# The residual addition on TensorE: an ordinary f32 matmul with a scaled diagonal in place of a transpose, and 1/ALPHA taken out of the branches

## The reference

```python
x = layer_norm(ALPHA * x + y, ln_mix_g[l], ln_mix_b[l])   # y: HGRN2 + convolution, or pooling
x = layer_norm(ALPHA * x + y, ln_xa_g[l], ln_xa_b[l])     # y: attention to a memory
x = layer_norm(ALPHA * x + y, ln_ffn_g[l], ln_ffn_b[l])   # y: swiglu
# ALPHA = 4 ** 0.25, layer_norm with an epsilon of 1e-5
```

## Time and profile before

| | |
|---|---|
| three runs | 1280.35, 1280.9, 1282.54 us, median 1280.9 |
| profiled execution | 1280.35 us, its span 1278.4 us |
| mean granted clock of PE | 0.996 |
| busy | PE 1258.9, DVE 829.3, ACT 661.1, POOL 27.6 us |
| instructions | 17136, of which 6788 matmul records of PE |
| read from HBM | 215.71 MB, 170 GB/s over the span |

### The profile page before, as it was taken

One profiled execution on the slowest core, in us unless ns is written; L12 is line 12 of the kernel. 1 busy time (PEld: TensorE's weight loads), 2 busy tenths in 40 slices (PEclk: granted clock), 3 DMA queues, 4 the chain that ended last, 5 costly groups with the idle time before them and its releaser, 6 DMA issues.

```text
span 1278.4 us, 17136 instructions
## 1 busy us (share of the span) xinstructions
PE 1258.9 (98%) x6788; PEld 1084.9 (85%) x6788; DVE 829.3 (65%) x1270; ACT 661.1 (52%) x999; POOL 27.6 (2%) x32
## 2 busy tenths in 40 slices
PE   9999999999999999999999999999999999999997
PEld 7888888898788888899989897888888997888886
DVE  5655666868667565667998665755557564755554
ACT  6454546657474444454525654644444654644443
POOL 0000000010000000000000000000001000000000
PEclk9999999999999999999998999999999999999999
DMA  8655555552355555554424542755555442655551
GB/s 288 216 184 182 182 189 189 166 181 83 104 181 186 183 192 185 185 173 151 152 83 149 193 137 88 260 189 190 192 186 165 165 149 83 217 195 189 189 185 62
DMA packets 61854, 217.87 MB, mean 170 GB/s; under 512 B 6608, under 2 KB 9936, under 8 KB 61264
## 3 DMA queue, kind: packets, MB, share of 16 engines
q1 hardware_dynamic: 61488, 216.29, 50.2%
q10 hardware_dynamic: 288, 0.49, 0.1%
HBM read 215.71 MB, written 1.05 MB: 170 GB/s over the span
## 4 chain that ended last, share of the span: by engine, by line
PE 90%; DVE 7%; ACT 1%; DMA 1%; issue 0%; SPq 0%; POOL 0%; DVEq 0%; ACTq 0%
PE bank L1920 27%; PE bank L1922 26%; PE bank L1921 26%; DVE arena L1740 3%; DVE w_lo L1117 2%; PE bank L2122 2%; PE bank L2259 1%; PE bank L2219 1%; PE bank L1942 1%; DMA w_raw<-weights_d 1%; PE bank L2230 1%; PE bank L2008 0%; PE bank L2042 0%; PE bank L2251 0%; PE bank L2213 0%
## 5 line engine op out<-in xcount | busy, mean ns | idle before, releaser
L1117 DVE TENSOR_TENSOR w_lo<-w_raw,w_hi 128x1024 fp32r<-128x1024 f32 x383 | 467.2, 1225 | 340.7 <-ACT w_hi L584 339.4
L584 ACT ACTIVATE w_hi<-w_raw 128x1024 fp32r<-128x1024 f32 x383 | 403.8, 1058 | 473.4 <-PE bank L1922 453.3
L1920 PE MATMUL bank<-w_hi,x_hi 128*128 128x512 f32 (+2 forms) x928 | 360.3, 388 | 2.9 <-DVE w_lo L1117 2.4
L1922 PE MATMUL bank<-w_hi,x_lo 128*128 128x512 f32 (+2 forms) x928 | 355.8, 383 | 0.0
L1921 PE MATMUL bank<-w_lo,x_hi 128*128 128x512 f32 (+2 forms) x928 | 355.6, 383 | 0.0
L1920 PEld LDWEIGHTS bank<-w_hi,x_hi 128*128 128x128 f32 x928 | 174.5, 188 | 37.4 <-DVE w_lo L1117 3.5
L1922 PEld LDWEIGHTS bank<-w_hi,x_lo 128*128 128x128 f32 x928 | 174.4, 188 | 34.0
L1921 PEld LDWEIGHTS bank<-w_lo,x_hi 128*128 128x128 f32 x928 | 174.6, 188 | 32.6
L1920 PE MATMUL bank<-w_hi,h_hi 128*128 128x512 f32 (+1 forms) x364 | 142.4, 391 | 0.0
L1922 PE MATMUL bank<-w_hi,h_lo 128*128 128x512 f32 (+1 forms) x364 | 141.3, 388 | 0.0
L1921 PE MATMUL bank<-w_lo,h_hi 128*128 128x512 f32 (+1 forms) x364 | 141.2, 388 | 0.0
(11 more groups left out here) (314 smaller groups left out, 1425.7 us busy)
## 6 DMA issues: line engine op xcount, KB each, us to landing
w_raw<-weights_d SPq DMA_DIRECT2D x395, 512.0 KB, 3.3
arena<-weights_d SPq DMA_DIRECT2D x4, 512.0 KB, 6.1
arena<-ln_rows_d SPq DMA_DIRECT2D x2, 1024.0 KB, 5.6
arena<-late_d SPq DMA_DIRECT2D x1, 1056.0 KB, 5.7
xs<-x_d SPq DMA_DIRECT2D x2, 512.0 KB, 6.1
kv_mem<-mem_d SPq DMA_DIRECT2D x1, 1024.0 KB, 8.7
out_d<-xs SPq DMA_DIRECT2D x4, 256.0 KB, 2.4
cst<-cst_d SPq DMA_DIRECT2D x1, 671.0 KB, 6.9
```

Source lines behind the costliest of these rows:

```text
L584: nc.scalar.activation(w_hi[:, slot(b), :], w_raw[:, b % RAW, :], ACT.Copy).then_inc(hi_ready, 1)
L1117: nc.vector.tensor_tensor(w_lo[:, slot(b), :], w_raw[:, b % RAW, :], w_hi[:, slot(b), :].bitcast(F32), ALU.subtract).then_inc(lo_ready, 1)
L1920: nc.tensor.matmul(out, wh, xh, start=start, stop=False, skip_group_check=True)
L1922: return nc.tensor.matmul(out, wl, xh, start=False, stop=stop, skip_group_check=True)
```

## The change

`residual` and the pooling branch use an ordinary f32 matmul with `res_i`, the identity times ALPHA, as moving operand. DVE makes `res_i` once at the start, and PE waits for it once, ahead of branch 5. All divisions by ALPHA go, with the two columns and their semaphore, and the epsilon is the plain one everywhere. The tensor `scaled` (16 columns) goes and `res_i` (128 columns) comes in its place in SBUF.

```diff
--- before.py
+++ after.py
@@ -188,7 +188,7 @@
         h_lo = sb("h_lo", [P, 8, S], F32R)
 
         tokst = sb("tokst", [P, 76])
-        scaled = sb("scaled", [P, 16])
+        res_i = sb("res_i", [P, P])[:]
         ident = sb("ident", [P, P])[:]
 
         kv_mem = sb("kv_mem", [P, 4, DC * S])
@@ -224,7 +224,6 @@
         row_sum = [small[:, 8 + 4 * k:12 + 4 * k] for k in range(2)]
         lam_e, lam_p, neg_lam = small[:, 16:18], small[:, 18:20], small[:, 20:21]
         g_q_scaled, g_sub_scaled = small[:, 21:22], small[:, 22:23]
-        hg_over, pool_over = scaled[:, 0:4], scaled[:, 4:12]
         lb_e, lb_t, lower, upper = small[:, 28:40], small[:, 40:44], small[:, 44:48], small[:, 48:52]
         decay = small[:, 56:88]
 
@@ -354,8 +353,8 @@
             "xt_ready xt_ps ss_ready rs_ready dg_ready rb_ps rb_ready")
         raw_in = [sem(f"raw_in{k}") for k in range(RAW)]
         hi_ready, lo_ready, block_done, vec_chain = sems("hi_ready lo_ready block_done vec_chain")
-        res_ready, xh_ready, xl_ready, y_ready, na_ready, nd_ready, xn_ready, xd_ready, over_alpha = sems(
-            "res_ready xh_ready xl_ready y_ready na_ready nd_ready xn_ready xd_ready over_alpha")
+        res_ready, xh_ready, xl_ready, y_ready, na_ready, nd_ready, xn_ready, xd_ready, id_scaled = sems(
+            "res_ready xh_ready xl_ready y_ready na_ready nd_ready xn_ready xd_ready id_scaled")
         lat_sq, var_ready, lat_norm, lat_t, lat_hi, lat_lo, v_up, vup_evac, dv_evac = sems(
             "lat_sq var_ready lat_norm lat_t lat_hi lat_lo v_up vup_evac dv_evac")
         dq_sq, dq_sum, dq_n, dq_t, dq_evac, dk_sq, dk_n, dk_t, dk_evac = sems(
@@ -768,7 +767,7 @@
                         done(b)
                         nc.scalar.activation(v_mem[l][:, :, c * S:(c + 1) * S],
                                              fill_bank(l, m, c)[:, :].rearrange("p (t n) -> p t n", n=S),
-                                             ACT.Copy, scale=1.0 / ALPHA).then_inc(mem_evac, 1)
+                                             ACT.Copy).then_inc(mem_evac, 1)
 
             def exponentials(n, head):
 
@@ -1068,12 +1067,11 @@
             blk()
             ln_norm(7, 1)
             mem_blocks(1, 8, 9)
-            act.wait_ge(over_alpha, 1)
             for c in range(DC):
                 act.wait_ge(pool_ps, 2 * (c // 4) + c % 2 + 1)
                 if c % 4 >= 2:
                     act.wait_ge(pool_lo, c - 1)
-                nc.scalar.activation(x_hi[:, c, :], pooled(c), ACT.Copy, scale=pool_over[:, c:c + 1]).then_inc(pool_hi, 1)
+                nc.scalar.activation(x_hi[:, c, :], pooled(c), ACT.Copy, scale=col("ln_g", LN_COL[7] + c)).then_inc(pool_hi, 1)
             for k in range(4):
                 act.wait_ge(xt_ps, 16 + 4 * LN[7] + k + 1)
                 x_pair(7, k)
@@ -1408,8 +1406,7 @@
             def ln_stats(v, t):
                 link(ln_part(v, 1, t))
                 link(nc.vector.bn_aggr(ln_mv[t], ln_bn[t]))
-                eps = LN_EPS if v in (7, 10) else LN_EPS / ALPHA ** 2
-                nc.vector.tensor_scalar(ln_var[:, t:t + 1], ln_mv[t][:, 1:2], eps, None, ALU.add).then_inc(var_ready, 1)
+                nc.vector.tensor_scalar(ln_var[:, t:t + 1], ln_mv[t][:, 1:2], LN_EPS, None, ALU.add).then_inc(var_ready, 1)
 
             def ln_norm(v, t):
 
@@ -1545,8 +1542,8 @@
             mark(nc.vector.tensor_scalar(g_q_scaled, col("g_diff_q"), SCALE_DIFF, None, ALU.mult))
             mark(nc.vector.tensor_scalar(g_sub_scaled, col("g_diff_sub"), 1.0 - LAMBDA_INIT, None, ALU.mult))
 
-            mark(nc.vector.tensor_scalar(hg_over, col("hg_g", 0, 4), 1.0 / ALPHA, None, ALU.mult))
-            nc.vector.tensor_scalar(pool_over, col("ln_g", LN_COL[7], DC), 1.0 / ALPHA, None, ALU.mult).then_inc(over_alpha, 1)
+            dve.wait_ge(x_in[0], 32)
+            nc.vector.tensor_scalar(res_i, ident, ALPHA, None, ALU.mult).then_inc(id_scaled, 1)
             token_ffn(0, FIRST["ffn1"])
             blk()
             token_rstd(1)
@@ -1848,7 +1845,7 @@
 
             for h in range(HG_HEADS):
                 dve.wait_ge(ho_bc, h // 2 + 1)
-                nc.vector.scalar_tensor_tensor(ho[:, h, :], ho[:, h, :], hg_over[:, h:h + 1], half(1 - h // 2, h),
+                nc.vector.scalar_tensor_tensor(ho[:, h, :], ho[:, h, :], col("hg_g", h), half(1 - h // 2, h),
                                                ALU.mult, ALU.mult).then_inc(hy_f, 1)
 
             for h in range(HG_HEADS):
@@ -1858,8 +1855,7 @@
             for k in range(CC + 1):
                 if k < CC:
                     dve.wait_ge(conv_ln, k + 1)
-                    nc.vector.scalar_tensor_tensor(conv[:, k, :], conv[:, k, :], 1.0 / ALPHA, conv_sig_buf[:, k, :],
-                                                   ALU.mult, ALU.mult).then_inc(cy_f, 1)
+                    nc.vector.tensor_tensor(conv[:, k, :], conv[:, k, :], conv_sig_buf[:, k, :], ALU.mult).then_inc(cy_f, 1)
                 if k:
                     c = k - 1
                     dve.wait_ge(cy_hi, c + 1)
@@ -1881,10 +1877,9 @@
             token_ffn(2, FFN3)
             blk()
             mem_blocks(8, 9)
-            dve.wait_ge(over_alpha, 1)
             for c in range(DC):
                 dve.wait_ge(pool_hi, c + 1)
-                low_gain(x_lo[:, c, :], pooled(c), pool_over[:, c:c + 1], x_hi[:, c, :], pool_lo)
+                low_gain(x_lo[:, c, :], pooled(c), col("ln_g", LN_COL[7] + c), x_hi[:, c, :], pool_lo)
             mem_blocks(9, 10)
             mark(ln_part(8, 0, 0))
             ln_stats(8, 0)
@@ -2005,8 +2000,8 @@
 
                 for t in range(2):
                     for c in range(4 * h, 4 * h + 4):
-                        nc.tensor.matmul(PB[banks[t]][:, c % 4 * P:c % 4 * P + P], xs[:, c, 0, t * P:(t + 1) * P], ident,
-                                         start=False, stop=False, is_transpose=True, skip_group_check=True)
+                        nc.tensor.matmul(PB[banks[t]][:, c % 4 * P:c % 4 * P + P], xs[:, c, 0, t * P:(t + 1) * P], res_i,
+                                         start=False, stop=False, skip_group_check=True)
 
             def token_turns(blocks, outs, chunks, hi, lo, start, stop, first=None, ready=None, between=None, ahead=0):
 
@@ -2573,6 +2568,7 @@
                     ins = nc.tensor.transpose(half(4 + c // 2, c)[:, t * P:(t + 1) * P], xs[:, c, 1, t * P:(t + 1) * P], ident)
                 if c % 2:
                     ins.then_inc(conv_t, 1)
+            pe.wait_ge(id_scaled, 1)
             token_out(5, AB_OUT, "ab_out", lambda c: pe.wait_ge(hy_lo, c + 1) if c < 4 else pe.wait_ge(cy_lo, c - 3), lambda i: None)
             mem_blocks(1, 6, 7)
             ln_turn_halves(5)
@@ -2614,8 +2610,8 @@
                         ins.then_inc(block_done, 1)
                 pe.wait_ge(xn_ready, XN[7] + DC)
                 for c in range(DC):
-                    ins = nc.tensor.matmul(PB[Z_BANK[8][c // 4][t]][:, c % 4 * P:c % 4 * P + P], xs[:, c, 0, s], ident,
-                                           start=False, stop=c % 4 == 3, is_transpose=True, skip_group_check=True)
+                    ins = nc.tensor.matmul(PB[Z_BANK[8][c // 4][t]][:, c % 4 * P:c % 4 * P + P], xs[:, c, 0, s], res_i,
+                                           start=False, stop=c % 4 == 3, skip_group_check=True)
                 ins.then_inc(zt_ps, 1)
             nb[0] += 2
             mem_blocks(1, 10, 14)
```

## The result

The changed kernel takes 1287.16 us in the median (1286.42 to 1287.82, 5 runs) against 1280.35 us for the kernel before in the same set of runs (1278.85 to 1282.54, 5 runs). The ratio is 1.0055, with a 95% interval of 1.0042 to 1.0069: slower, by 6.8 us in the medians. The forecast was 1288.2 us, range 1285.5 to 1290.5. The profiled execution of the changed kernel took 1286.86 us; its span is 1284.8 us. Ten further executions of the changed kernel are on record and in none of these figures: nine lie between 1285.22 and 1290.64 us, and one took 5632.21 us, for which I have no cause.

A forecast was written before the change was run, and what follows sets the result against it. The prediction took PE, busy 98% of the span, as the bound. Eight residual groups add 7.3 us, all other terms nothing: 1280.35 + 7.3 = 1287.65, plus 0.55 to the runs' median, 1288.2 us, range 1285.5 to 1290.5.

The forecast's parts named there:

- The unit: PE's residual additions: 8 ordinary matmuls take 1.78 us against 0.87 for 8 transposes, 0.91 extra a group, 7.3 for eight.
- The prediction's lower bound: PE's residual matmuls: a record can hardly be cheaper than 0.106 us, so 64 more cost at least 6.8 us.
- All on the path: All eight residual groups lie on PE's part of the chain, from 699.29 to 1063.71 us, so 7.3 us counts in full.
- Nothing back: PE's longer waits after 699 us, 3.5 us for x_lo and 3.2 for ACT, shift without shrinking; nothing is regained.
- Rival A: PE waits less for x_lo after the first group and regains up to 3.5 us, giving 1284.7 us; chance 0.06.
- The rule: Skill pages: FP32 transpose mode four times as fast, true FP32 matmul four passes; the prediction set a trace factor of two against it.
- Rival B: Residual matmuls on PE cost four transposes each, 20.9 us more, giving 1301.8 us; chance 0.03.
- DVE and ACT: Making the diagonal, dropped small operations and constants, convolution products and gains change the time by nothing, 0.12 us if cover is gone.
- rival D: The arena's move makes the convolution's taps on DVE cheaper, so the kernel is faster, for example 1277.2 us; chance 0.03.
- the sum: Whole kernel: 1280.35 + 7.3 = 1287.65 us for the profiled execution, 1288.2 for the median.
- a sign against it: The prediction is wrong if the span before 699 us, ahead of the first residual group, moves.

The follow-up runs named there:

- Experiment 1: Kernel before with only the 64 residual transposes made ordinary f32 matmuls with the plain identity; 1286.45 us, ratio 1.0048.
- experiment 3: Changed kernel with each of the 64 ordinary residual matmuls issued twice; 1300.6 us, ratio 1.0161 to the kernel before.
- experiment 4: Changed kernel with the residual matmuls in f32r, 128 wide, on a tile of the memory's high part (wrong tensor added); 1279.52 us, ratio 0.9998 to the kernel before.
- experiment 2: Changed kernel with the 64 residuals put back to transposes with the identity, the rest of the change kept; 1279.64 us, ratio 1.0002 to the kernel before.
- Experiment 5: Kernel before, no edit, run again for a second profile; 1278.32 us, one run.
- experiment 7: Changed kernel with 12 spare matmuls at the end and 8 and 5 in two waits for w_lo in the convolution's stretch; 1286.42 us, ratio 1.0059 to the kernel before.
- experiment 8: Kernel before, with its transposes, plus spare matmuls at the end and in two convolution waits; 1277.69 us, ratio 0.9995.
- experiment 6: Changed kernel with 12 spare 128x128 f32 matmuls in PE's wait at the end; 1286.31 us, ratio 1.0061 to the kernel before.

## Why the prediction was right

**The unit.** 8 ordinary matmuls at 1.78 us against 8 transposes at 0.87 was read from one stretch of another line and holds to the hundredth on the residual lines. Experiment 1 shows that this edit makes the cost, experiment 3 that it adds up (0.223 for a further one), and experiment 4 that one record of 128 columns in f32r costs no less than a transpose. The prediction's lower bound, that a record can hardly be cheaper than 0.106 us, is too general: in the same trace the 14 records of L2527, on 32 partitions, take from 654.18 to 654.83 us, 0.046 each. For the residuals, which fill 128 partitions, it holds.

**All on the path.** The eight groups lie on the chain at 1.78 us each, but for the first of the pool branch (2.05 for 1.08 before), the statistics of branch 5 stand 1.82 us later behind the first, and between the cuts the kernel is 7.5 us longer for the 7.3 forecast: 7.1 from the matmuls (experiment 1), 0.3 to 0.4 from the rest (experiment 2), which I had at nothing.

**Nothing back.** PE's waits are the same after, and the same with three times the delay (experiment 3). Rival A is out.

**The rule.** The Trainium skill has the transpose mode as four times as fast for FP32 (TensorE: Matmul & The Clock Gate, section Terms). This case's traces don't agree: the factor is two on the residual lines, 1.78 us for 0.87, as it was on L2501. The Trainium skill's four passes of a true FP32 matmul (FP8 and Floating Point Precision, section TensorE Precision Notes) aren't contradicted by it: at 256 columns the two f32 records take 0.43 us against 0.12 for an f32r matmul, a factor of 3.6. Rival B took a transpose for the unit of those four, and a transpose of 128 columns stands at the floor, as an f32r matmul of as many columns does (experiment 4).

**DVE and ACT.** The diagonal's making takes 0.22 us for 0.285 by the nearest row, and the next w_lo starts at 20.15. The products of the convolution take 0.418 with and without the constant. The taps take 0.481 for 0.478, so rival D had nothing behind it. Nothing of this shows in the time (experiment 2), as forecast.

**What the sum missed.** The absolute time, by 1.0 us. The median of before that I started from was 1280.9; with two more runs it was 1280.35, and 1280.35 + 7.3 = 1287.65 against 1287.16. The medians differ by 6.8 us for the 7.3 forecast; the ratio's interval, taken as time, runs from 5.4 to 8.8 us, so the whole time can't tell the two apart, and that it came out within 0.5 us is in part luck. The 7.3 rest on the stretch between the cuts. The prediction named a move of the span ahead of 699 us as a sign against it. That stretch did move, by 1.3 us, and the statistics of branch 5 came at 720.63 for 722.0 by it. Experiment 5 shows that it moves so in the unchanged kernel: the sign was badly chosen, since one profile can't tell such a move from the scatter.

## What to carry to other kernels

On PE, count records, and look at their shape. With operands on 128 partitions, a 128-column operation costs about 0.11 us as a transpose, as an f32r matmul, and for each of the two records of an ordinary f32 matmul; fewer columns are no cheaper, 256 columns of f32 cost twice as much for each record, and operands on 32 partitions took less than half. So a transpose that also accumulates is the cheap form of an addition, and a scale folded into it doubles its price; fold the scale into an operation on an engine with time to spare, as the kernel before does. Where PE is the bound and the other engines wait for it, a delay on PE adds up in full: look whether PE's waits follow its own work before counting anything as given back. To compare two profiles, cut the span at instructions that both have: here the stretch between the cuts repeats to 0.2 us where the whole differs by 2.

## What the runs showed that I had not expected

The granted clock falls in the convolution's stretch in seven of the eight profiles that have no fillings there, at one of three places or at several, between 644 and 690 us. In the first profile of the kernel before it was at 1.2 GHz, half of 2.4, for most of 680 to 688 us:

```profile
682.00:684.00 2.00, 2.00 (x11) 0.50 0.86 274
684.00:686.00 2.00, 2.00 (x11) 0.50 0.71 233
```

PE had issued thin matmuls before it (L2544 with 32 columns, L2550 with one) and waited for 0.8 us up to 674.4. The profile of experiment 2 has the same drop and its first group at the same 699.1. In other profiles there was no drop (experiment 3, and experiments 7 and 8 with their fillings), one of half the length (experiments 1, 5 and 6), or three (experiment 4, whose first group therefore starts at 701.5 for 696.2 in experiment 3). The scatter of the runs goes with it. On the chip of experiments 1 to 4 the kernel before took 1277.15 us at a mean clock of 0.998, 1278.4 to 1280.2 at 0.996, and 1282.3 to 1282.7 at 0.993. Filling two waits of PE there and the one at the end with wide matmuls left a clock of 1.00 through the stretch in both profiles and a mean of 0.998 or 0.999 in all 16 runs, where 13 of 15 runs without were at 0.997 or less. With the end alone filled (experiment 6) three of five were at 0.998, and the profile has its drop at 674 to 678 us. This speaks for the waits having a part in it, but doesn't show it, since experiment 3's profile has no drop without any filling. Whether the thin matmuls have a part too wasn't tried. In the medians the fillings gave 1.2 us at most.
